# Layer one of a two-layer attention trunk: values of all heads computed first and kept on chip, running sums added onto the scores in PSUM

## What is computed

```python
h = rms_norm(x, g[0])
q, k, v = split(h @ w_qkv)                        # (heads, 256, 64) each
z = q @ k.T * 64 ** -0.5
strict = key_pos < query_pos
log_stay = where(strict, log_sigmoid(-z), 0.0)    # -softplus(z)
# after[s] = log_stay[s + 1], summed from the far end:
log_a = log_sigmoid(z) + reverse_cumsum(after)
a = where(strict, exp(log_a), 0.0)
x = x + rms_norm((a @ v) @ w_o, g[1])
```

## Time and profile before

| what | value |
|---|---|
| median of 3 runs | 788.68 us (787.62 to 788.86) |
| the profiled execution's own time | 787.89 us |
| its span, first to last instruction | 786.2 us |
| around the span | 1.69 us |
| PE busy | 777.0 us, 99% of the span |
| DVE, ACT, GpSimd busy | 497.7, 374.8, 104.5 us |
| mean granted TensorE clock | 0.998 |

### The profile page before, as it was taken

The page is one execution under the profiler, slowest core; times in us unless marked ns, Lnnn a source line. Parts: engine busy times, 40 slices in busy tenths (PEclk is TensorE's granted clock), DMA queues, the critical chain, the costliest instruction groups (busy, mean ns, idle before and its releaser), DMA issues.

```text
span 786.2 us, 13014 instructions
## 1 busy us (share of the span) xinstructions
PE 777.0 (99%) x4773; PEld 684.9 (87%) x4773; DVE 497.7 (63%) x632; ACT 374.8 (48%) x452; POOL 104.5 (13%) x141
## 2 busy tenths in 40 slices
PE   8999999999999999999999999999999999999996
PEld 7999978888888888999999999999988888888885
DVE  6888987774554556876746647557547655564553
ACT  5665667543434434934544445445356433433321
POOL 2000001100000000354414215223102000000000
PEclk9999999999999999999999999999999999999999
DMA  7534965766645555569567576585622865656602
GB/s 230 166 113 130 285 190 187 240 227 215 201 160 180 193 171 158 152 173 245 139 169 192 130 193 155 141 217 174 214 87 89 305 216 165 207 164 213 210 1 53
DMA packets 160514, 138.65 MB, mean 176 GB/s; under 512 B 6105, under 2 KB 150081, under 8 KB 160481
## 3 DMA queue, kind: packets, MB, share of 16 engines
q1 hardware_dynamic: 157536, 131.55, 54.5%
q0 software_dynamic: 2688, 6.35, 4.0%
q10 hardware_dynamic: 256, 0.30, 0.1%
HBM read 137.07 MB, written 1.11 MB: 176 GB/s over the span
## 4 chain that ended last, share of the span: by engine, by line
PE 97%; DVE 2%; ACT 1%; issue 0%; DVEq 0%; POOLq 0%; POOL 0%; ACTq 0%
PE ps L1117 20%; PE ps L1119 20%; PE ps L1118 19%; PE ps L1123 9%; PE ps L1125 9%; PE ps L1124 9%; PE ps L1363 2%; PE ps L1396 2%; PE ps L1384 2%; PE ps L1265 1%; PE ps L1194 1%; PE ps L1205 1%; PE ps L1172 1%; PE ps L1138 1%; DVE w_lo L726 1%; PE ps L1425 1%
## 5 line engine op out<-in xcount | busy, mean ns | idle before, releaser
L726 DVE TENSOR_TENSOR w_lo<-raw,w_hi 128x2048 fp32r<-128x2048 f32 (+2 forms) x144 | 284.8, 1996 | 33.6 <-ACT w_hi L464 31.9
L464 ACT ACTIVATE w_hi<-raw 128x2048 fp32r<-128x2048 f32 (+2 forms) x144 | 232.3, 1637 | 63.3 <-DMA raw<-in_w_kv_b 21.6
L1117 PE MATMUL ps<-w_hi,xt 128*128 128x512 f32 x352 | 139.5, 396 | 0.0
L1119 PE MATMUL ps<-w_hi,xt 128*128 128x512 f32 x352 | 137.3, 390 | 0.0
L1118 PE MATMUL ps<-w_lo,xt 128*128 128x512 f32 x352 | 137.1, 389 | 0.0
L605 ACT ACTIVATE work<-ps,stat 128x256 f32<-128x256 f32 x44 | 21.0, 476 | 201.4 <-PE ps L1119 201.4
L1123 PE MATMUL ps<-xt,w_hi 128*128 128x256 f32 x384 | 110.3, 287 | 0.7 <-DVE w_lo L1018 0.7
L1124 PE MATMUL ps<-xt,w_hi 128*128 128x256 f32 x384 | 108.5, 283 | 0.0
L1125 PE MATMUL ps<-xt,w_lo 128*128 128x256 f32 x384 | 108.5, 283 | 0.0
L1117 PE MATMUL ps<-w_hi,ot 128*128 128x512 f32 x240 | 94.8, 395 | 0.4 <-DVE w_lo L726 0.2
L1119 PE MATMUL ps<-w_hi,ot 128*128 128x512 f32 x240 | 93.5, 390 | 0.0
(11 more groups left out here) (127 smaller groups left out, 1148.2 us busy)
## 6 DMA issues: line engine op xcount, KB each, us to landing
raw<-in_w_gate_up SPq DMA_DIRECT2D x88, 512.0 KB, 4.8
raw<-in_w_kv_b SPq DMA_DIRECT2D x96, 256.0 KB, 3.8
raw<-in_w_down SPq DMA_DIRECT2D x22, 1024.0 KB, 4.9
raw<-in_w_q_b SPq DMA_DIRECT2D x48, 256.0 KB, 4.1
raw<-in_w_qkv_a SPq DMA_DIRECT2D x23, 512.0 KB, 4.9
raw<-in_w_o_a SPq DMA_DIRECT2D x4, 1024.0 KB, 5.5
work<-bias_rows POOLq DMA_DIRECT2D x64, 64.0 KB, 4.2
raw<-in_w_o_b SPq DMA_DIRECT2D x4, 1024.0 KB, 4.8
```

The source lines that it names most:

```text
L464: act.activation(w_hi[:, s % CUT, 0:size(s)], raw[:, s % RAW, 0:size(s)], ACT.Copy).then_inc(hi_made, 1)
L726: dve.tensor_tensor(w_lo[:, c, 0:n], raw[:, s % RAW, 0:n], w_hi[:, c, 0:n].bitcast(F32), ALU.subtract).then_inc(lo_made, 1)
L1117: mm(out, xs[0], ws[0], start=start, stop=False)
L1119: return mm(out, xs[1], ws[0], start=False, stop=stop)
```

## The change

The order of layer one's attention becomes: first the values of all heads, then Q and K pair by pair.

- Values: units 0 to 3 are now 256 rows of the V weights by all 1024 columns each (1 MB, loaded and split by rows of 512 KB, the first in parts). PE's `values_a(t, k)` streams 512 weight columns against 128 tokens (`by_x`), 2 token tiles by 8 k by 2 halves by 3 passes, with the transposes of x's second tile between them. `take_v` on ACT copies the four banks into `va` with the norm's factor. V is not transposed any more, and `take_v_a`, `turn_v` and the copy L540 go.
- Q and K: units 4 to 19, two for each pair, Q into bank 0, K into bank 1. `take_q_a` and `take_k_a` are separate steps of DVE.
- Scores of even and odd pairs lie in banks 3, 4 and 5, 6. The triangular matrix is negated and includes the diagonal, so that the sums added by PE onto the scores in the same bank give the logarithm of the weights; DVE's `arg` and `stay_a` go. `sums_a` is made per head: two matmuls of 384 columns and two of 128 (`ones_r`), with fp32r operands. The exponential reads PSUM, on ACT behind the next pair's absolute value.
- Order on PE in `step_a(p)`: half of Q, scores of p-1, sums of p-2, the rest of Q, half of K, outputs of p-2, the rest of K.
- Start: 3 `keep_busy` in place of 5, 3 in place of 4; the sums of squares later on DVE. The loops of layer one are written out.

Below, added lines and lines around them; the lines that they replace stand in the kernel before.

```diff
+VA0 = 0
+VA = KT // 2
+QA0 = VA0 + VA
+WOA0 = QA0 + 2 * PAIRS
...
+    later = -(i[:, None] >= i[None, :]).astype(np.float32)
...
+            def pair_a(p):
+                for c in range(2):
+                    load(QA0 + 2 * p + c, 0, lambda r: r.rearrange("p (k n) -> p k n", k=KT),
+                         qkv_dram[:, c, :, P * p:P * p + P])
+            def values_a(u, rows_=range(2)):
+                for r in rows_:
+                    if u >= RAW and r == 0:
+                        sp.wait_ge(lo_made, u - RAW + 1)
+                    sp.dma_start(raw[:, u % RAW, D * r:D * r + D], v_dram[:, 2 * u + r, :]
+                                 ).then_inc(landed[u % RAW] if r else row_in[u % RAW], 16)
...
             sp.dma_start(eye[:, :], square[:, 0, :]).then_inc(eye_in, 16)
...
+            sp.dma_start(xn[:, 0, :], x_dram[0]).then_inc(x_in[0], 16)
+            sp.dma_start(raw[:, 0, 0:HALF], v_dram[:, 0, 0:HALF]).then_inc(part_in, 16)
+            sp.dma_start(raw[:, 0, HALF:D], v_dram[:, 0, HALF:D]).then_inc(row_in[0], 16)
+            sp.dma_start(xn[:, 1, :], x_dram[1]).then_inc(x_in[1], 16)
+            values_a(0, [1])
+            values_a(1)
+            values_a(2)
             sp.dma_start(ones[:, :], square[:, 3, :]).then_inc(ones_in, 16)
             sp.dma_start(select_in[0:BUCKETS, :], select).then_inc(bias_in, 16)
             sp.dma_start(rel_in[0:BUCKETS, :], rel_bias).then_inc(bias_in, 16)
             sp.dma_start(later, square[:, 1, :]).then_inc(later_in, 16)
...
+            for n in range(2):
+                sp.dma_start(strict[:, P * n:P * n + P], square[:, 2, :]).then_inc(strict_in, 16)
+            values_a(3)
+            for p in range(PAIRS):
+                pair_a(p)
...
+            def weights_a(a):
+                act.wait_ge(r_done, a + 1)
...
+                    act.wait_ge(pva_done, a)
+                act.activation(wts, banks(z_banks(a), 2, WA), ACT.Exp).then_inc(wts_made, 1)
+            def attend_a(a, units):
+                act.wait_ge(z_done, a + 1)
+                if a >= 1:
+                    act.wait_ge(spl_made, a)
+                act.activation(ell, banks(z_banks(a), 2, WA), ACT.Abs).then_inc(abs_made, 1)
+                if a >= 1:
+                    weights_a(a - 1)
+                act.wait_ge(abs_made, a + 1)
...
+                hi(units[0])
+                act.wait_ge(spl_masked, a + 1)
...
+                    act.wait_ge(r_done, a)
                 act.activation(spl_cut[0], spl, ACT.Copy).then_inc(spl_hi, 1)
...
+                if len(units) > 1:
+                    hi(units[1])
...
+            def take_v(t):
+                act.wait_ge(*((w_used, VA) if t else (v_done, 1)))
+                act.wait_ge(bias_done, 1)
+                act.wait_ge(xrs_made, t + 1)
+                for half in range(2):
+                    cols = slice(HALF * half, HALF * half + HALF)
+                    act.activation(va[t][:, cols], bank(2 * t + half), ACT.Copy, scale=x_rs(0, t)).then_inc(va_made, 1)
...
+            cut_x0(1, 3)
+            hi_row(3, 1)
+            act.wait_ge(later_in, 16)
+            act.wait_ge(ones_in, 16)
+            act.activation(later_r, later, ACT.Copy)
+            act.activation(ones_r, ones[:, :], ACT.Copy, scale=-1.0).then_inc(exact_made, 1)
+            for u in range(QA0, QA0 + 3):
+                hi(u)
+            for t in range(NT):
+                take_v(t)
+            for u in range(QA0 + 3, QA0 + 7):
+                hi(u)
+            for a in range(PAIRS - 1):
+                attend_a(a, (QA0 + 2 * a + 7, QA0 + 2 * a + 8))
+            attend_a(PAIRS - 1, (FA0 + 1,))
+            weights_a(PAIRS - 1)
...
+                if a >= 1:
+                    dve.wait_ge(spl_hi, a)
+                dve.scalar_tensor_tensor(spl, banks(z_banks(a), 2, WA), 0.0, ell, ALU.max, ALU.add).then_inc(spl_made, 1)
+                dve.wait_ge(spl_made, a + 1)
+                dve.tensor_tensor(spl[:, :, P:WA], spl[:, :, P:WA], strict2, ALU.mult).then_inc(spl_masked, 1)
+            def cut_softplus_a(a):
+                dve.wait_ge(spl_hi, a + 1)
                 dve.tensor_tensor(spl_cut[1], spl, spl_cut[0].bitcast(F32), ALU.subtract).then_inc(spl_cut_made, 1)
...
+            def mask_a(a):
+                dve.wait_ge(wts_made, a + 1)
+                dve.scalar_tensor_tensor(wts[:, :, P:WA], wts[:, :, P:WA], LARGEST, strict2, ALU.min, ALU.mult
+                                         ).then_inc(wts_masked, 1)
+            def take_q_a(p):
+                dve.wait_ge(w_used, QA0 + 2 * p + 1)
                 if p >= 1:
...
+                    dve.wait_ge(z_done, p)
+                dve.scalar_tensor_tensor(qa.rearrange("p (t n) -> p t n", t=NT), swapped(bank(0, 0, SEQ)), SCALE,
+                                         swapped(rows[:, :]), ALU.mult, ALU.mult).then_inc(qa_made, 1)
+            def take_k_a(p):
+                dve.wait_ge(w_used, QA0 + 2 * p + 2)
+                dve.tensor_tensor(ka, bank(1, 0, SEQ), rows[:, :], ALU.mult).then_inc(ka_made, 1)
+            def step_a(p):
+                if p >= 1:
+                    take_k_a(p - 1)
+                lo(QA0 + 2 * p + 3)
+                lo(QA0 + 2 * p + 4)
                 if p >= 2:
...
+                    mask_a(p - 2)
+                take_q_a(p)
+                if p >= 1:
+                    softplus_a(p - 1)
+                if p >= 2:
+                    outputs_a(p - 2)
+                if p >= 1:
+                    cut_softplus_a(p - 1)
...
+            squares_of(0)
+            lo_row(2, 1)
+            cut_x0(0, 3)
+            squares_of(1)
+            lo_row(3, 0)
+            cut_x0(1, 3)
+            lo_row(3, 1)
             take_rows(1)
...
             dve.wait_ge(bias_done, 1)
...
+            dve.tensor_copy(bias_out[0:NH, :], ps[0:NH, 7 * 512:8 * 512]).then_inc(bias_out_made, 1)
+            dve.wait_ge(strict_in, 32)
+            for u in range(QA0, QA0 + 3):
+                lo(u)
+            for p in range(PAIRS):
+                step_a(p)
+            take_k_a(PAIRS - 1)
+            mask_a(PAIRS - 2)
...
+            def project_a(p, c, ks=range(KT)):
+                s = QA0 + 2 * p + c
+                pe.wait_ge(lo_made, s + 1)
+                if p >= 1:
+                    pe.wait_ge(ka_made if c else qa_made, p)
                 w = cut_unit(s, k=KT)
                 for k in ks:
...
+            def values_a(t, k):
+                u, row = k // 2, k % 2
+                w = cut_unit(u, k=2)
+                pe.wait_ge(xt_made, 4 * (k // 2) + 2 * t + k % 2 + 1)
+                for half in range(2):
+                    if u == 0 and half == 0:
+                        pe.wait_ge(part_lo, row + 1)
+                    else:
+                        pe.wait_ge(lo_made if row else row_lo, u + 1)
+                    inst = by_x(bank(2 * t + half), [xt[:, n, k, P * t:P * t + P] for n in range(2)],
+                                [v[:, row, HALF * half:HALF * half + HALF] for v in w], k == 0, k == KT - 1)
+                if t == 0 and k == KT - 1:
+                    inst.then_inc(v_done, 1)
+                if t == 1 and row:
+                    inst.then_inc(w_used, 1)
...
+            def sums_a(a):
+                pe.wait_ge(spl_cut_made, a + 1)
+                for hh in range(2):
+                    b = z_banks(a) + hh
+                    for n in range(2):
+                        mm(bank(b, 0, WA), later_r, spl_cut[n][:, hh, :], start=False, stop=False, skip_group_check=True)
+                    for n in range(2):
+                        inst = mm(bank(b, 0, P), ones_r, spl_cut[n][:, hh, SEQ:WA], start=False, stop=n == 1,
+                                  skip_group_check=True)
+                inst.then_inc(r_done, 1)
+            def outputs_a(a):
                 if a >= 1:
...
+                    pe.wait_ge(ot_made, a)
+                pe.wait_ge(wts_masked, a + 1)
...
+            def step_a(p):
+                first, second = range(KT // 2), range(KT // 2, KT)
+                project_a(p, 0, first)
+                if p >= 1:
+                    scores_a(p - 1)
                 if p >= 2:
...
+                    sums_a(p - 2)
+                project_a(p, 0, second)
+                project_a(p, 1, first)
+                if p >= 2:
+                    outputs_a(p - 2)
+                project_a(p, 1, second)
...
+            keep_busy(3)
             pe.wait_ge(eye_in, 16)
             pe.wait_ge(gain_in_s, 16 * 2)
...
+            pe.transpose(bank(2, 0, 9 * KT), gain_in[0:9 * KT, :], eye[0:9 * KT, 0:9 * KT]).then_inc(gain_done, 1)
+            def turn_x(t, b):
                 pe.wait_ge(x_in[t], 16)
...
+                if t:
+                    pe.wait_ge(xt_made, 4 * b + 2)
+                for k in (2 * b, 2 * b + 1):
+                    inst = pe.transpose(x_block(k, t), xn[:, t, P * k:P * k + P], eye[:, :])
+                inst.then_inc(xt_done, 1)
```

(79 more changed lines are left out.)

336 lines of the change are left out of this document (98 added, 238 removed).

## The result

The changed kernel takes 795.17 us (median of 6 runs, 794.69 to 795.65), the kernel before 788.07 us (median of 6, 787.62 to 788.86). The ratio is 1.0089, 95% interval 1.0076 to 1.0102: slower by 7.1 us. The profiled execution's own time is 794.92 us, its span 793.2 us. The whole difference has arisen by the end of out_proj.

The account below looks back on a forecast made before the run. The prediction took PE's own row of instructions, busy 777.0 of 786.2 us, as the bound. Its terms -1.5 - 1.2 - 1.8 - 0.5 + 1.2 + 1.0 + 4.9 + 6.4 gave 787.9 + 8.5 = 796.4 us, range 789.9 to 800.5.

Parts of the forecast that it names:

- the new waits: PE waiting in layer one for hand-overs, mostly DVE's remainders and take-overs: +6.4 us in all.
- Removed work: On PE, V's transposes go, -1.5 us, and V's projection becomes 96 matmuls of 512 columns, -1.2 us.
- the breaks and transposes added: On PE, x's second-tile transposes among the values, with three breaks, +1.2 us; six more breaks for outputs, +1.0 us.
- The start: Values begin near 7.8 us where projections began at 9.64: -1.8 us; a 0.5 us wait there goes too.
- the two risks named: At the start, PE's array still at 1.2 GHz, or x's second tile late behind 512 KB more: 0 to +2 us.
- The narrow sums: 128-column fp32r products in `sums_a`, priced as plain fp32 at 0.19 to 0.21 us each: +4.9 us, bounds +0.2 and +4.9.
- rival A: 128-column sums products run in one pass at 0.115 us each: 1.8 in place of 4.9, total 793.3 us; chance 0.22.
- the rule of 0.107 us: Loading weights takes their column count over 1.2 ns, whatever streams: 0.107 us per 128-column sums product, sum 3.1 us lower.
- The 1.0 at the scores of pair 1: PE waits 1.0 us because the scores-to-scores cycle takes 7.7 us against PE's own step of 6.8.
- the 0.3 at the last sums: Sums of the last pair come 0.3 us late behind DVE's last out_proj remainder.
- the long wait: Ahead of pair 1, PE waits 2.9 us for Q of pair 0, taken behind late-loaded units 7 and 8.
- The rival that PE never waits (D): From the values to pair 2 PE never waits, and narrow products cost 0.066 to 0.115 us: 786.1 us; chance 0.08.

Follow-up runs that it names:

- e1: Changed kernel with DVE taking Q of pair 0 ahead of the remainders of units 7 and 8, K of pair 0 between them: 794.32 us.
- e4: Changed kernel with DVE making the remainders of units 4 and 5 ahead of taking the spread rows: 789.75 us, ratio to before 1.0016.
- e6: e4 plus DVE taking K of pair p before the softplus remainder of p-1, and PE making the last scores before the previous pair's sums: 788.43 us.
- e7: e6 plus PE making the outputs of pair p-3 directly ahead of the scores of pair p-1: 788.10 us, ratio to before 0.9998.
- e3: Changed kernel with x's second tile issued ahead of the first weight row, as in the kernel before: 794.83 us.
- e9: e8 plus x's second tile issued between the first two pieces of weights: 788.45 us, ratio to before 1.0006.
- e5: Kernel before with only the two 256-column ones-matrix products of the sums made into four of 128 columns: 789.84 us, ratio 1.0019.
- e2: Changed kernel with PE running 14 idle products where it waited for Q of pair 0: 793.96 us, ratio to before 1.0072.
- e8: e7 plus ACT taking the first half of the values before unit 6's high part, and 5 idle products at PE's start, not 3: 787.47 us.

## Why the prediction was right, and where not

The forecast was 796.4 us in a range from 789.9 to 800.5; measured were 795.17 us, slower as forecast. The direction rests on the new waits, which e1 and e4 confirm. The terms, though, did not all have their size.

- **Removed work** (1.5 and 1.2 us) and the breaks and transposes added (1.2 and 1.0): as worked out. 90 value products with three breaks run from 8.86 to 30.31 us, 21.4 us, where the prices say 21.6. The break of the outputs is 0.18 us by the steps of e6 and e7. No run measured the other terms by themselves; together they can be read from the steps, 11.66 us before and 8.93 after, 2.73 less, where V's projection, V's transposes, one more break and the dearer sums say 2.62.
- **The start**, -1.8 forecast, -0.8 measured (9.64 to 8.86 us). Of the two risks named it was x's second tile; e3 and e9 show that neither of two other orders of the first loads avoids it. The clock was the other, and it came true in executions of e1, e4, e6 and e7.
- **The narrow sums**, +4.9 forecast, +2.2 measured (1.20 in place of 0.93, eight times). This step failed: I took the plain fp32 row for the nearest, and rival A was right, with a block of 1.15 us in e5 and here 1.20, of which 0.04 are a slower first half behind the fp32 scores. The 128-column transposes in the earlier trace rows, from which A's 0.115 us came, have both widths in common with these products; which of the two sets the price no run parted. And where the prediction says that by the rule of 0.107 us the sum would lie 3.1 us lower, it has worked with 0.115; 0.107 gives 3.4.
- **The waits**, +6.4 forecast, +5.2 measured: 1.1 for 1.1, 3.1 for 2.9, 1.0 for 1.1. The 1.0 at the scores of pair 1 (0.9 by the prediction's own figures, 7.7 less 6.8) and the 0.3 at the last sums didn't show: the half-rate stretch hid the first. In e2, without that stretch, it is there with 0.8. The way of the long wait, through the loads of units 7 and 8, is what e1 and e4 confirm.
- **The clock behind the wait**, not in the sum, +2.7. I had seen the slow first products and applied them to the start only; the sum put the clock behind a wait at nothing without a reason, and the waits of 3.0 to 3.1 us, here, in e1 and in e3, all carried it. With A in place of the dear sums and the start as measured, the sum would have been 794.3 with nothing for the clock.

The measured terms: -0.8 - 0.5 - 1.5 - 1.2 + 1.2 + 1.0 + 2.2 + 5.2 + 2.7 = +8.3 us, against 7.1. 0.7 of the 1.2 lie in out_proj: from its first product to the transposes it takes 24.07 us (110.15 to 134.22) where before took 24.51 (102.57 to 127.08), and one narrow block should have added 0.27; why it is shorter stays open. The rest is as much as the scores' blocks became shorter, which no term had: 0.86 us where the earlier trace rows has 0.93, seven times. So the forecast was as near as it was partly because the narrow sums, too dear by 2.7, stood in for the clock, which was left out. That was luck: the two errors are equal in size and have nothing to do with each other.

That the waits would reach their end through the loads was the useful part of the argument. The rival that PE never waits (D) had as its condition that units 7 and 8 are split by 38.8 us; e4 came near it by another road. They are split by 39.2 us, the wait for Q is gone, three waits of 2.3 us in all remain, and the time came down to 789.75 us.

## What to carry to other kernels

When the last engine's row is full, follow each new hand-over from the last thing that releases it, through the loads too: the two lines of DVE's order that were worth 5.4 to 5.8 us stood 7 us ahead of the wait that they caused. Price a wait of the bounding engine with what its clock does behind it, and fill it with idle products where it can't be removed. The nearest row for a narrow matmul was here the one with both of its widths (0.115 us), not the one with its type, and its price is read over the whole block, since the start distances of the narrow ones alone (0.08 to 0.10) leave out what they cost the product behind. Where times are too noisy for an effect of 0.2 us a step, the length of the steps in two traces shows it.

## What the runs showed of the hardware

- In the changed kernel a wait of PE of 3.1 us brought the granted clock down to 0.50, 2.4 us after PE had come to stand, and it stayed there for 6.1 us of dense work behind the wait: 2.7 us lost on 3.1 waited. In e1, with a wait as long, it fell only 0.6 us after work had resumed and stayed down for 3.4 us. Single waits of 0.8 and 1.1 us left it at 1.00 (e2, e4). In e7 two waits of 1.2 and 0.6 us with 0.9 us of work between them were followed by 3.4 us at 0.50.
- fp32r products with 128 streamed columns start 0.08 to 0.10 us apart, against 0.12 for 256; over the whole block of e5 each costs 0.11 us.
- A plain fp32 block among fp32r projections costs 0.18 us for the break (steps of 8.93 us in e6, 8.75 in e7).
- With the same idle products at the start, broken by 0.6 to 1.1 us of standing, the array was at full rate for x's transposes in three profiles and at half rate in four, 1.0 to 1.2 against 1.9 us for eight of them. Without the pause it was at full rate in the kernel before, e8 and e9, and nearly so in e5 (1.4 us).
